# One hybrid attention and state-space layer on one core: head loads on another queue, bias strips built in another stage, and a head loop whose steps sit one chunk later

## What is computed

```python
h = rmsnorm(x, pre_norm_g)
proj = h @ w_in                                  # 2048 x 13376 weights
q, k, v, z_attn, z_ssm, xbc, dt_raw = jnp.split(proj, cuts, axis=-1)
o = dilated_attention(q, k, v, rel_bias_table)   # 16 heads of 128
attn_out = rmsnorm(o) * silu(z_attn)
xbc = silu(conv5(xbc)); xs, bm, cm = split(xbc)  # 32 heads of 64, 4 groups of state 128
dt = softplus(dt_raw + dt_bias)
y = ssd_scan(xs, dt, a, bm, cm) + ssd_scan(reversed) + d_skip * xs
ssm_out = rmsnorm_by_group(y * silu(z_ssm))
return x + rmsnorm(concat([attn_out, ssm_out]) @ w_out, post_norm_g)
```

## Time and profile before

| | us |
|---|---|
| median of 3 runs (2744.78 to 2747.74) | 2746.18 |
| the profiled execution | 2744.54 |
| its span, first to last instruction | 2742.8 |
| PE busy in the span | 2557.5 (93%) |
| DVE busy | 1544.8 (56%) |
| ACT busy | 870.2 (32%) |

### The profile page before, as it was taken

The page is one execution under the profiler, slowest core; times in us unless marked ns, Lnnn a source line. Parts: engine busy times, 40 slices in busy tenths (PEclk is TensorE's granted clock), DMA queues, the critical chain, the costliest instruction groups (busy, mean ns, idle before and its releaser), DMA issues.

```text
span 2742.8 us, 37581 instructions
## 1 busy us (share of the span) xinstructions
PE 2557.5 (93%) x14004; PEld 2390.9 (87%) x14004; DVE 1544.8 (56%) x2388; ACT 870.2 (32%) x1409; POOL 0.2 (0%) x4
## 2 busy tenths in 40 slices
PE   6998489999999999999999999999999699999998
PEld 6997489999999999888898888888888588888887
DVE  5543375555555544665556666666655665544447
ACT  5321133333333333333333333333333421111113
POOL 0000000000000000000000000000000000000000
PEclk9998799999999999999999999999999899999999
DMA  4333423333333344344444433344444332222215
GB/s 154 94 106 118 131 72 104 89 105 101 92 107 96 99 143 148 127 136 132 141 126 141 131 123 108 121 130 141 137 137 133 111 140 93 86 85 99 84 62 200
DMA packets 287844, 320.81 MB, mean 117 GB/s; under 512 B 15030, under 2 KB 232310, under 8 KB 283303
## 3 DMA queue, kind: packets, MB, share of 16 engines
q1 hardware_dynamic: 279783, 298.59, 34.2%
q10 hardware_dynamic: 8000, 21.38, 2.1%
HBM read 271.76 MB, written 55.51 MB: 119 GB/s over the span
## 4 chain that ended last, share of the span: by engine, by line
PE 73%; DMA 11%; DVE 6%; SPq 3%; ACT 3%; issue 3%; DVEq 0%; ACTq 0%
PE ps L855 23%; PE ps L926 19%; PE ps L660 19%; DMA w_raw<-in_w_in 10%; PE ps L640 5%; PE ps L780 2%; PE ps L808 2%; PE ps L763 2%; ACT stage L1116 1%; DVE stage L1631 1%; ACT w_hi L1003 1%; DVE stage L1652 1%; SPq L360 1%; SPq L409 1%; SPq L445 1%
## 5 line engine op out<-in xcount | busy, mean ns | idle before, releaser
L1395 DVE TENSOR_TENSOR w_lo<-w_raw,w_hi 128x512 fp32r<-128x512 f32 x244 | 167.6, 690 | 531.1 <-ACT w_hi L1003 523.7
L660 PE MATMUL ps<-h_hi,w_hi 128*128 128x384 f32 x1536 | 409.1, 347 | 3.3 <-issue 3.3
L660 PE MATMUL ps<-h_lo,w_hi 128*128 128x384 f32 x1536 | 396.7, 339 | 0.0
L1003 ACT ACTIVATE w_hi<-w_raw 128x512 fp32r<-128x512 f32 x240 | 150.0, 627 | 775.8 <-PE ps L660 467.1
L660 PE MATMUL ps<-h_hi,w_lo 128*128 128x384 f32 x1536 | 395.3, 338 | 0.0
L926 PE MATMUL ps<-h_hi 128*128 128x512 f32 x768 | 300.5, 391 | 3.7 <-issue 3.7
L926 PE MATMUL ps<-h_lo,h_hi 128*128 128x512 f32 x768 | 299.4, 390 | 0.0
L926 PE MATMUL ps<-h_hi,h_lo 128*128 128x512 f32 x768 | 299.4, 390 | 0.0
L660 PEld LDWEIGHTS ps<-h_hi,w_hi 128*128 128x128 f32 x1536 | 278.7, 193 | 8.1 <-issue 3.7
L660 PEld LDWEIGHTS ps<-h_lo,w_hi 128*128 128x128 f32 x1536 | 283.2, 191 | 0.0
L660 PEld LDWEIGHTS ps<-h_hi,w_lo 128*128 128x128 f32 x1536 | 282.5, 191 | 0.0
(11 more groups left out here) (226 smaller groups left out, 3927.4 us busy)
## 6 DMA issues: line engine op xcount, KB each, us to landing
w_raw<-in_w_in SPq DMA_DIRECT2D x240, 256.0 KB, 3.0
raw_qk<-in_w_in SPq DMA_DIRECT2D x66, 512.0 KB, 3.9
stage<-in_w_out SPq DMA_DIRECT2D x30, 1024.0 KB, 5.0
stage<-cb_scr SPq DMA_DIRECT2D x16, 1664.0 KB, 13.7
stage<-loc_scr SPq DMA_DIRECT2D x16, 1536.0 KB, 8.2
stage<-zx_scr SPq DMA_DIRECT2D x32, 384.0 KB, 3.0
stage<-er_scr SPq DMA_DIRECT2D x32, 384.0 KB, 9.8
u_scr<-stage ACTq DMA_DIRECT2D x32, 384.0 KB, 3.3
```

The source lines that it names most:

```text
L660: last = nc.tensor.matmul(ps[:, 2 * parity + b, 0:HALF_T], w, h[:, k * T + b * HALF_T:k * T + (b + 1) * HALF_T], start=(k == 0 and p == 0) ...
L1003: nc.scalar.activation(w_hi[:, c, :], w_raw[:, c, :], ACT.Copy).then_inc(w_hi_done, 1)
L1395: nc.vector.tensor_tensor(w_lo[:, c, :], w_raw[:, c, :], w_hi[:, c, :].bitcast(f32), ALU.subtract).then_inc(w_lo_done, 1)
```

## The change

The change moves work between stages, queues and slots.

- SP's queue: the dt tile's weights are loaded first (behind a wait for a DVE memset of the unused half of `w_raw`, `w_zeroed`), then those of B and C. Seven of the eight strip copies move from between the window tiles' weight loads to the start of pairs 1 to 7 of the block products. The `y12_scr` stores move to ACT's queue, right behind the dt tile. All loads of a head move from SP's queue to ACT's; SP issues nothing but weights in the head loop.
- PE, DVE, ACT: the dt tile is made first, and its chain (`dt_and_adt`, `dt_cumulate`, `locs_and_coefs`, `rows_and_coefs`) runs beside group 0. The last group's convolution and `cb_prompt` run beside the window tiles, at steps 0 to 3. `t_step` runs at steps 1, 4 and 5 in place of 4, 5 and 6. Its buffers lie elsewhere in `stage`.
- Head loop: the softmax's transposes move from slot 2 to 3, and everything behind them by one slot as well; `y` is gated in step 10 and not 9, and ACT issues the next head's `zs` and decay loads there. In the last iteration `decay_exponents` and its exponential move into the steps after the loop.

The core of the diff:

```diff
+            sp.wait_ge(w_zeroed, 1)
             for c in range(NCH):
-                load_w(c, COL_B, c)
+                load_w(c, COL_DT, c, width=64)
...
-                if m % 2 and m + 1 < HEADS:
-                    make_strips(m + 1, strip_out[1])
-                if m == 9:
-                    for q, h in enumerate((h_hi, h_lo)):
-                        sp.dma_start(y12_scr[q * P:(q + 1) * P, :].rearrange("p (k t) -> p k t", k=HK),
-                                     h_block(h, 0, 1).bitcast(f32)).then_inc(y12_out, 16)
...
             pair_transfers(0)
-            with sp.Fori(1, NP - 1) as p:
+            for n in range(HEADS // 2 - 1):
+                make_strips(2 * n + 2, strip_out[1])
+                pair_transfers(n + 1)
+            with sp.Fori(HEADS // 2, NP - 1) as p:
                 pair_transfers(p)
...
-            def iteration(i, a):
+            with sp.Fori(0, HEADS - 1) as a:
                 for m in range(IT_CHUNKS):
                     j, c = divmod(m, NCH)
-                    if m == 1:
-                        load_z(za, ZX_ZA, a, za_in, att_gated, a + 1)
-                    if m == NCH:
-                        sp.wait_ge(w_lo_done, chunk_of(i, m) - NCH + 1)
-                        load_heads(a)
-                    load_w(chunk_of(i, m), i * P + LOOP_COLS[j], c, waited=(m == NCH))
-                    if m == 9:
-                        load_strip(i)
-                load_xs(i)
+                    load_w(chunk_of(a + 1, m), a * P + (P + LOOP_COLS[j]), c)
...
             def cb_prompt(g):
 
                 pe.wait_ge(bc_silu, 2 * g + 2)
+                pe.wait_ge(loc_read, 1)
+                pe.wait_ge(rows_read, 2)
+                pe.wait_ge(coef_exp, 1)
...
-                if a is not None and s == 2:
+                if a is not None and s == 3:
                     pe.wait_ge(normed, 6 * a + 4)
...
-                if a is not None and s == 9:
+                if a is not None and s == 10:
                     pe.wait_ge(off_read, 2 * a + 1)
                     pe.wait_ge(wmat_done, a + 1)
...
+            act.wait_ge(h_lo_done, 2 * KT)
+            for q, h in enumerate((h_hi, h_lo)):
+                act.dma_start(y12_scr[q * P:(q + 1) * P, :].rearrange("p (k t) -> p k t", k=HK),
+                              h_block(h, 0, 1).bitcast(f32)).then_inc(y12_out, 16)
             bc_steps(0, None)
...
+            def load_decays(a):
+                act.dma_start(decay.rearrange("p (d n) -> p d n", d=2),
+                              loc_scr.rearrange("(d h) t -> d (h t)", d=2)[:, ds(a * 2 * T, 2 * T)]
+                              .partition_broadcast(P)).then_inc(decay_in, 16)
+                for h in range(2):
+                    act.dma_start(er[64 * h:64 * h + 64, :].rearrange("p (d n) -> p d n", d=2),
+                                  er_scr.rearrange("(d h) t -> d (h t)", d=2)[:, ds(a * 2 * T + h * T, T)]
+                                  .partition_broadcast(64)).then_inc(er_in, 16)
+                act.dma_start(cb, cb_scr[ds((a // 4) * P, P), :]).then_inc(cb_in, 16)
...
                 if a is not None and s == 10:
-                    act.wait_ge(y_gated, a + 2)
+                    act.wait_ge(y_gated, a + 1)
                     act.dma_start(u_scr[ds((a + HEADS) * P, P), :], y).then_inc(ys_stored, 16)
-                if i is not None and s == 10:
+                    if i is not None:
+                        load_gate(zs, ZX_ZS, i, zs_in)
+                        load_decays(i)
+                if i is not None and s == 11:
+                    tile_ready(tile_of(i, K))
+                    tile_hi(parity_of(ip, K), k_hi, 1.0)
...
+                if i is not None:
+                    decay_exponents(a)
...
-                    if final and s == 9:
-                        dve.wait_ge(y_gated, i + 1)
+                    if final and s == 10:
+                        dve.wait_ge(y_gated, i)
                         columns_of_channels(i)
                         columns_of_heads(i)
                         settle()
                         convolve_xs(i)
-                        decay_exponents(i)
```

More of the change, by code:

```diff
@@ L392, in _ @@
                              ).then_inc(row_in, 16)
-            for c in range(NCH):
-                load_w(3 * NCH + c, COL_C + P, c)
-            with sp.Fori(2, SSM_GROUPS) as g:
+            for c in range(2, NCH):
+                load_w(2 * NCH + c, COL_C, c)
+            sp.wait_ge(brow_out, 16)
+            make_strips(0, strip_out[0])
+            with sp.Fori(1, SSM_GROUPS) as g:
                 gcol = sp.snap(g * P)
@@ L398, in _ @@
                     for c in range(NCH):
[L399 to L435, removed]
+                        load_w(NCH + 2 * NCH * g + NCH * j + c, gcol + base, c)
             for m in range(WIN * NCH):
@@ L690, in bc_tiles @@
                         cb_sample(post)
[L692 to L697, removed]
             def dt_transposes():
                 pe.wait_ge(dt_out, 1)
-                pe.wait_ge(pcb_read, 5 * (SSM_GROUPS - 1) + 2)
+                pe.wait_ge(brow_read, 2)
                 for c in range(TT):
@@ L736, in dt_cumulate @@
                 last.then_inc(cum_ready, 1)
+            pe.wait_ge(h_lo_done, KT + 10)
+            for half in range(2):
+                gemm_half(0, 0, 0, half)
+                if half == 0:
+                    pe.wait_ge(h_lo_done, 2 * KT)
+                    biases_by_distance()
+            bc_tiles(0, None)
+            with pe.Fori(0, SSM_GROUPS - 1) as g:
+                bc_tiles(g + 1, g)
             QK_PASSES = ((q_hi, k_hi), (q_hi, k_lo), (q_lo, k_hi))
@@ L1124, in step @@
                                              accum_out=lsum[:, PCH + t:PCH + t + 1]).then_inc(probs_exp, 1)
-                if a is not None and s == 2:
-                    for b in range(2):
-                        act.wait_ge(pt_ready, 4 * a + b + 1)
-                        nc.scalar.activation(pT[:, b * SEQ:(b + 1) * SEQ], ps[:, 4 + b, :], ACT.Copy
-                                             ).then_inc(pt_out_act, 1)
+                if a is not None and i is None and s == 1:
+                    exp_of_decays(a)
                 if i is not None and s == 3:
@@ L1134, in step @@
                 if a is not None and s == 3:
+                    for b in range(2):
+                        act.wait_ge(pt_ready, 4 * a + b + 1)
+                        nc.scalar.activation(pT[:, b * SEQ:(b + 1) * SEQ], ps[:, 4 + b, :], ACT.Copy
+                                             ).then_inc(pt_out_act, 1)
+                if a is not None and s == 4:
                     act.wait_ge(pts_ready, a + 1)
@@ L1489, in bc_steps @@
                             cb_out(post, True)
+            for s in range(2):
+                for m in (2 * s + 4, 2 * s + 5):
+                    split_lo(m, m % NCH)
+                if s == 0:
+                    biases_out()
+                if s == 1:
+                    zero_pads()
             bc_steps(0, None)
```

382 lines of the change are left out of this document (192 added, 190 removed).

## The result

The changed kernel takes 2686.86 us (median of 4 runs, 2686.07 to 2687.50), the kernel before 2746.96 beside it: a ratio of 0.9773 with a 95% interval of 0.9748 to 0.9799, that is 60 us less. 2626 had been predicted, with a range of 2574 to 2670. The direction was right; half of the gain is missing, and the time lies outside the range.

What follows compares the result with a forecast made beforehand. PE was taken to bound almost everything except the window stage, head loop and stretch behind it. Terms -63 + 47 - 102 - 2 = -120 took 2744.54 to 2624.5; the median, 1.64 higher, gave 2626, range 2574 to 2670.

Steps and rivals of the forecast that it cites:

- Window stage, -63: Window stage: without strip copies and `y12` stores, the first pair's fifth half starts at 302.4, not 365.97; bounds -74 to -53.
- Strips in the pairs, +47: Block products: in seven pairs a copy delays `store_c2`, ACT waits at the snapshot, PE loses 6.7 us each.
- The +70 bound: Block products: upper bound of the strips' cost, if all of ACT's 9 to 10 us wait reaches PE.
- Head loop, -102: Head loop: loads off SP's queue end the late weights and PE's stalls; 102 us less, bounds -106 to -50.
- 13 x 7.07: Head loop: 13 head intervals each fall from 73.43 to 66.36 us, 91.9 us in all.
- Loads on ACT, nothing with 1.2 us to spare: Head loop, steps 10 and 11: issuing loads on ACT costs nothing, about 7.8 us of work against some 9.
- Tail, -2: Behind the head loop: idle before the last scores shrinks, mostly repaid by the decay exponents; 2 us less, -8 to +6.
- C: Head loop: keeps half of its stall as loads share the same DMA engines; 2677 us, chance 0.18.
- B: Block products: the strip copies are hidden in the pairs, all of +47 goes; 2576 us, chance 0.12.
- D: Head loop: ACT is held while issuing head loads, making the kernel slower than before; 2771 us, chance 0.03.
- E: Window stage: gains 25 us less because DVE becomes its bound; 2651 us, chance 0.05.

Runs made afterwards that it cites:

- both repairs: The changed kernel with the strip copies on ACT's queue and DVE's loop eight instructions further on: 2579.71 us, ratio 0.9375 to the kernel before.

## Why the prediction was wrong

*Window stage, -63: right.* 61.7, with the fifth half at 304.26 for a predicted 302.4. PE idles 4.73 us just before it, and ACT waits for no weights there. That the strips were the cause is shown by the kernel in which they alone moved.

*Strips in the pairs, +47: the mechanism right, the term too small.* 61.5 for the stage, of which 4.5 are the slower pace of every pair, that stays without the copies (639.42) and had no term; 57.0 are the copies'. The place was as forecast: ACT at the snapshot, seven pairs and no other. The store landed where the sum had it: 345.1 is 21.6 us after the issue of `store_c1` at 323.49, for a predicted 494 - 472.73 = 21.3. But PE idled 5.5 us a pair on average (38.8 over seven) where I had taken 4.5, the lower end, and the lower granted clock cost 2.6 us a pair (PE busy 657.65 for 639.42 with both repairs, over seven) where 2.2 had been carried over from two shorter stalls. The +70 bound held.

*Head loop, -102: the failed step.* 55.8. What the step says of the weights is right: with only the head's loads moved a head is 67.76 us, and with the later slots and no fetch 66.15; the loop then gains 104.2 us (1153.30 to 1049.10), for 102. Wrong is what it takes for granted in 13 x 7.07, that with the weights on time nothing else is late in any head. At the jump of DVE's loop its program was fetched anew, and PE waited for DVE, in six of the thirteen intervals, 49.6 us together over 66.15 each. The position of the loops had no place in the sum; an instruction ahead of a loop was counted at nothing, as if it cost only its own time. No row of the kernel before shows such a fetch in the loop, so its price wasn't to be read there; the edit that brings it (one more instruction ahead of the loop) was in the diff.

*Loads on ACT, nothing with 1.2 us to spare: right.* In a head without a fetch ACT waits 1.30 us for PE at its second split behind the loads (1126.74), and DVE 1.41 us for the scores in the rows of the kernel with DVE's loop shifted by eight.

*Tail, -2: right in size,* 2.5 for all that stands behind the loop.

With the terms as they were measured the sum is -61.7 + 61.5 - 55.8 - 2.5 in place of -63 + 47 - 102 - 2. Of the 60.9 us between 2626 and 2686.9 the head loop is 46, the pairs 14.5 (10 of them the copies').

*The rivals.* C came near in its time, 2677, and its sign came on average (69.96 us from head 1 to head 14), by luck: with the loads on the same engines the stall goes when DVE's program is moved. The Trainium skill's rule behind C (a second issuer saves only the time to issue) gave 2682, also near by luck: with the fetch gone the loop gains 104 us, not 46. B fell (PE did stop in the pairs), D and E didn't come.

## What to carry to other kernels

A loop that an engine keeps from pass to pass without fetching it may cease to be so when an instruction is added ahead of it, as DVE's did here, and the price shows where the loop jumps back: look at the instruction queues in the page's list of DMA queues, at idle time put down to "issue" behind a jump, and at stalls that return every pass and not every step. Ask what else a stall covers: in the kernel before with one instruction more, 9 us of late weights left 18 us of the fetches to be seen, and in the change, without them, they cost 50. A slow transfer is priced by what stands behind it in its own queue; the same copy, no shorter, gave back 53 us when the store was put ahead of it and 57 when it went to ACT's queue.

## What the runs showed of the hardware that was not expected

- One memset ahead of a loop of 263 DVE instructions made the kernel before 18 us slower. Of the starts tried, the one it makes and the one five further are bad, the ones just outside these and one two further still are good. In the change the bad start costs 50 us, 8.3 for each jump.
- The instruction packets on that queue are 8.2 KB (0.41 MB / 50), on the other one 16 KB (0.67 MB / 41). The Trainium skill ("Runtime: NRT & Kernel Launch", "Instruction fetch mechanics") says that an engine's buffer is a FIFO, that a jump to a place outside it stalls for a fetch, and that blocks are 16 KiB; the trace agrees with the stall at the jump, and not with the size on this queue. Its figure of 32 KiB for a buffer is four packets of 8.2 KB; it would fit that a loop in three packets stays and one in four doesn't, since the packet behind the loop's end is fetched too (five packets a pass). That last step is argued, not shown. In blocks of 16 KiB the loop would lie in two or in three, with the same bad starts, but packets of 8.2 KB would then come in pairs; five in each pass, one of them alone, speak for the smaller block.
- With a fetch DVE stood still for 7.3 and 4.2 us at one jump, for 1.75 and 1.41 without, though its packets are busy for 0.3 to 0.6 us each. The DMA engines were nine tenths busy with a head's loads then; whether that made it so long wasn't tried.
